# Layer 0's adaLN modulation: shift and scale by fp32 products at the start, the other 32 column tiles inside the attention

## The reference, cut to what matters

```python
def adaln(cond, w, b):
    m = (jax.nn.silu(cond) @ w + b)[..., None, :]
    return jnp.split(m, 6, axis=-1)          # w: 1024 x 6144, fp32, 25 MB
...
        mp = adaln(c_ctx, ada_w[layer], ada_b[layer])    # 128 context tokens
        ms = adaln(c, ada_w[layer], ada_b[layer])        # 512 latent tokens
        hp = modulate(yp, mp[0], mp[1])                  # x * (1 + scale) + shift
        hs = modulate(ys, ms[0], ms[1])
        if kind == 0:                                    # layers 0 and 3: latent attention
            op, ckv, kpe = mla_context(hp, *wts)
            os_ = mla_latent(hs, cache_ckv[:, j], cache_kpe[:, j], cos, sin, *wts)
        ...
        yp = layer_norm(ALPHA * yp + mp[2] * op, ln_g[layer, 0], ln_b[layer, 0])
        fp = swiglu(modulate(yp, mp[3], mp[4]), ffn_wg[layer], ffn_wu[layer], ffn_wd[layer])
        yp = layer_norm(ALPHA * yp + mp[5] * fp, ln_g[layer, 1], ln_b[layer, 1])
```

## Time and profile before

| | us |
|---|---|
| median of 3 runs | 3951.5 |
| the three runs | 3951.24, 3951.50, 3957.62 |
| span of the profiled execution | 3955.7 |

### The profile page before, as it was taken

The page is one execution under the profiler, slowest core; times in us unless marked ns, Lnnn a source line. Parts: engine busy times, 40 slices in busy tenths (PEclk is TensorE's granted clock), DMA queues, the critical chain, the costliest instruction groups (busy, mean ns, idle before and its releaser), DMA issues.

```text
span 3955.7 us, 74569 instructions
## 1 busy us (share of the span) xinstructions
PE 3625.6 (92%) x31532; PEld 3412.5 (86%) x31532; DVE 2466.1 (62%) x3517; ACT 938.1 (24%) x1804; POOL 1840.3 (47%) x875
## 2 busy tenths in 40 slices
PE   8999999999889778888999994899999989999998
PEld 3877799999788678888999994799998777899997
DVE  5366678758785466655885768886676566632125
ACT  5322231001244255532310012310013222220011
POOL 1311156665455646535566552466554101356663
PEclk9999999999999888889999997899999999999999
DMA  8200024333235543322343331243332000122221
GB/s 318 62 12 17 17 81 147 136 112 123 70 127 182 149 87 94 84 55 102 114 142 119 124 101 36 90 145 128 123 102 73 27 12 17 43 70 75 76 76 53
DMA packets 226844, 367.60 MB, mean 93 GB/s; under 512 B 104752, under 2 KB 111088, under 8 KB 226416
## 3 DMA queue, kind: packets, MB, share of 16 engines
q1 hardware_dynamic: 171408, 255.08, 20.9%
q10 hardware_dynamic: 55136, 107.98, 7.9%
HBM read 326.47 MB, written 36.54 MB: 92 GB/s over the span
## 4 chain that ended last, share of the span: by engine, by line
PE 71%; DVE 16%; issue 3%; ACT 3%; DMA 1%; SPq 1%; POOL 1%; ACTq 1%; DVEq 0%; POOLq 0%
PE ps L819 52%; PE ps L1091 3%; PE ps L1067 3%; DVE f_acc L2159 2%; PE ps L862 2%; PE ps L1077 2%; DVE m_mx L2390 1%; PE ps L1046 1%; DVE r_t L2456 1%; DVE x L2257 1%; DVE r_hlo L2440 1%; DVE ps L2605 1%; PE ps L1027 1%; DVE x L2266 1%; PE ps L879 1%
## 5 line engine op out<-in xcount | busy, mean ns | idle before, releaser
L674 POOL TENSOR_TENSOR w_hi<-w_raw,zrow 128x1024 fp32r<-128x1024 f32 x354 | 693.7, 1959 | 1783.6 <-PE ps L819 979.9
L676 POOL TENSOR_TENSOR w_lo<-w_raw,w_hi 128x1024 fp32r<-128x1024 f32 x354 | 900.2, 2543 | 27.8
L2159 DVE SCALAR_TENSOR_TENSOR f_acc<-f_unit,silu_c,f_acc 128x512 f32<-128x512 f32 x504 | 631.3, 1293 | 7.6
L819 PE MATMUL ps<-f_hhi,w_hi 128*128 128x320 f32 x2688 | 634.1, 317 | 0.0
L819 PE MATMUL ps<-f_hhi,w_lo 128*128 128x320 f32 x2688 | 613.0, 309 | 0.0
L819 PE MATMUL ps<-f_hlo,w_hi 128*128 128x320 f32 x2688 | 610.8, 308 | 0.0
L819 PEld LDWEIGHTS ps<-f_hlo,w_hi 128*128 128x128 f32 x2688 | 449.6, 188 | 0.0
L819 PEld LDWEIGHTS ps<-f_hhi,w_lo 128*128 128x128 f32 x2688 | 448.9, 188 | 0.0
L819 PEld LDWEIGHTS ps<-f_hhi,w_hi 128*128 128x128 f32 x2688 | 441.2, 188 | 0.0
L819 PE MATMUL ps<-f_ahi,w_hi 128*128 128x320 f32 x1408 | 322.2, 310 | 0.2 <-DVE f_alo L2304 0.2
L819 PE MATMUL ps<-f_alo,w_hi 128*128 128x320 f32 x1408 | 320.9, 309 | 0.0
(11 more groups left out here) (401 smaller groups left out, 6710.4 us busy)
## 6 DMA issues: line engine op xcount, KB each, us to landing
w_raw<-in_w SPq DMA_DIRECT2D x340, 512.0 KB, 3.5
f_unit<-in_ada_w ACTq DMA_DIRECT2D x72, 1024.0 KB, 5.8
ada_ring<-in_ada_w SPq DMA_DIRECT2D x24, 1024.0 KB, 6.6
up_scratch<-r_o ACTq DMA_DIRECT2D x40, 320.0 KB, 3.3
s_LW<-up_scratch SPq DMA_DIRECT2D x16, 320.0 KB, 5.1
s_LA<-up_scratch SPq DMA_DIRECT2D x8, 640.0 KB, 6.6
x<-in_x SPq DMA_DIRECT2D x1, 2560.0 KB, 9.4
x_scratch<-r_o ACTq DMA_DIRECT2D x8, 320.0 KB, 2.2
```

What stands on the lines that cost most here:

```text
L674: nc.gpsimd.tensor_tensor(whi[:, slot, :], raw[:, raw_slot, :], zrow[:, 0:1].to_broadcast([P, CH * P]), ALU.add).then_inc(w_hi_done, 1)
L676: nc.gpsimd.tensor_tensor(wlo[:, slot, :], raw[:, raw_slot, :], whi[:, slot, :].bitcast(F32), ALU.subtract).then_inc(w_split, 1)
L819: last = mm(ps[:, 2 * b + h, 0:HT], w, r[:, h * HT:(h + 1) * HT], start=kt == 0 and n < 2, stop=kt == KT - 1 and n >= 4)
L2159: last = stt(acc[:, cd, :], unit[:, k, :], by, acc[:, cd, :], ALU.mult, ALU.add)
```

## The change

The opening loads only the first 2048 of the matrix's 6144 columns (shift and scale): 8 units, each with its own buffer. They are not split: PE uses them as the stationary operand in plain fp32, 128 x 128 each, with silu(c), 2 columns wide, moving; that gives the result as columns and needs no turning. DVE adds the bias (and 1 to the scale), and ACT waits for that (`ada_mod`) and for x (`s_x`); the three barriers at the start are gone. x is loaded behind the 8 units and the first weight chunk.

The other 4096 columns are 32 tiles of 128 columns, four for each pair of the attention, each with 8 fp32 products (`late`). ACT issues their loads of 512 KB: three at the pair's beginning, the fourth after the first tile's products. PE multiplies tile 0 of a pair before `turn(0)`, tile 1 before `turn(5)`, tile 2 before `turn(9)` and tile 3 before `av(9)`. DVE copies the pair's 8 result columns behind its last copy of a transpose. `modulation(0)` runs on DVE after the loop.

```diff
-ADA_SLOTS, ADA_SPLITS = 4, 3
+EARLY = 2 * KD // 4
+LATE_AT = 2 * KD
+LATE_GROUPS = 4
+LATE_BUFFER = (0, 0, 1, 2)
+LATE_TURN, LATE_AV = (0, 5, 9), (10,)
...
             sp.dma_start(cst[:, :], a["cst"]).then_inc(s_const, 16)
-            sp.dma_start(x[:, :, :], a["x"].rearrange("k p t -> p k t")).then_inc(s_const, 16)
...
-            for u in range(ADA_UNITS):
-                slot = u % ADA_SLOTS
-                if u >= ADA_SLOTS:
-                    sp.wait_ge(ada_lo, u - ADA_SLOTS + 1)
-                sp.dma_start(m_ada.ring[slot][:, :, :],
+            for u in range(2 * EARLY):
+                sp.dma_start(m_ada.unit[u][:, :, :],
                              src[:, 4 * (u % 2):4 * (u % 2) + 4, (u // 2) * 512:(u // 2 + 1) * 512]
-                             ).then_inc(ada_land[slot], 16)
+                             ).then_inc(ada_land[u // 2], 16)
...
+                    pieces(LAYER_BASE[L], order, 0, 1)
+                    if L == 0:
+                        sp.dma_start(x[:, :, :], a["x"].rearrange("k p t -> p k t")).then_inc(s_x, 16)
+                    pieces(LAYER_BASE[L], order, 1)
...
-                for n in range(48):
-                    mm(ps[:, 6, 2 * n:2 * n + 2], m.rows[0:2, n * P:(n + 1) * P], ident[0:2, 0:2], start=True, stop=True)
-                end()
-                end()
+                pe.wait_ge(s_cond, 1)
+                for cb in range(EARLY):
+                    units = m_ada.unit[2 * cb:2 * cb + 2]
+                    pe.wait_ge(ada_land[cb], 32)
+                    for n in range(4):
+                        for k in range(KD):
+                            last = mm(ps[:, 6, 8 * cb + 2 * n:8 * cb + 2 * n + 2], units[k // 4][:, k % 4, n * P:(n + 1) * P],
+                                      sc_c[:, k, :], start=k == 0, stop=k == KD - 1)
+                last.then_inc(ada_mm, 1)
+
+            def late(j, p):
+
+                b = LATE_BUFFER[p]
+                pe.wait_ge(ada_land[b], j * 32 + 16 * (p + 3) if b == 0 else j * 16 + 48)
+                for k in range(KD):
+                    last = mm(ps[:, 7, 2 * p:2 * p + 2], m_mla[0].late[b][:, k, :], sc_c[:, k, :], start=k == 0, stop=k == KD - 1)
+                last.then_inc(late_mm, 1)
...
+                        if L == 0 and u in LATE_TURN:
+                            late(j, LATE_TURN.index(u))
                         if u < 10:
                             turn(u)
+                        if L == 0 and u in LATE_AV:
+                            late(j, len(LATE_TURN) + LATE_AV.index(u))
                         if u:
                             av(u - 1)
...
+                    act.wait_ge(s_x, 16)
+                    act.wait_ge(ada_mod, 1)
...
+                    act.dma_start(m.late[LATE_BUFFER[p]], late_src[:, :, bass.ds(j * (LATE_GROUPS * P) + (LATE_AT + p) * P, P)]
+                                  ).then_inc(ada_land[LATE_BUFFER[p]], 16)
...
+                    if L == 0:
+                        for p in (0, 2, 3):
+                            load_late(j, p)
                     for u in range(10):
                         qt = u % 5
+                        if L == 0 and u == LATE_TURN[0] + 2:
+                            act.wait_ge(late_mm, j * LATE_GROUPS + 1)
+                            load_late(j, 1)
...
+                ch(tt(mod[:, 0:LATE_AT, :], ps[:, 6, 0:2 * LATE_AT].rearrange("p (n c) -> p n c", c=2),
+                      adab[:, 0, 0:LATE_AT].unsqueeze(2).to_broadcast([P, LATE_AT, 2]), ALU.add))
+                s = mod[:, KD:2 * KD, :]
+                ts(s, s, 1.0, None, ALU.add).then_inc(ada_mod, 1)
...
+                    if L == 0:
+                        dve.wait_ge(late_mm, j * LATE_GROUPS + LATE_GROUPS)
+                        cp(mods[0][:, bass.ds(j * LATE_GROUPS + LATE_AT, LATE_GROUPS), :],
+                           ps[:, 7, 0:2 * LATE_GROUPS].rearrange("p (n c) -> p n c", c=2))
```

More of the change, by code:

```diff
@@ L241, in build @@
         sc_c = sb("silu_c", [P, KD, 2])
-        sc_hi, sc_lo = sb("silu_hi", [P, KD, 2], F32R), sb("silu_lo", [P, KD, 2], F32R)
         hmod, hmix = sb("hmod", [P, 2, KD, 2]), sb("hmix", [P, 2, KD, 2])
@@ L270, in build @@
         stage_end = sem("stage_end")
-        stage_free = sem("stage_free")
-        s_init, s_const = sem("s_init"), sem("s_const")
-        ada_land = [sem(f"ada_land{i}") for i in range(ADA_SLOTS)]
+        s_init, s_const, s_x, s_cond, s_eps = sem("s_init"), sem("s_const"), sem("s_x"), sem("s_cond"), sem("s_eps")
+        ada_land = [sem(f"ada_land{i}") for i in range(EARLY)]
         unit_land = [sem(f"unit_land{i}") for i in range(2)]
         unit_used, unit_sum, unit_col = sem("unit_used"), sem("unit_sum"), sem("unit_col")
-        ada_mm, ada_row, ada_hi, ada_lo = sem("ada_mm"), sem("ada_row"), sem("ada_hi"), sem("ada_lo")
+        ada_mm, ada_mod, late_mm = sem("ada_mm"), sem("ada_mod"), sem("late_mm")
         outs_done = sem("outs_done")
@@ L289, in f_ada @@
         def f_ada(m, g):
-            m.rows = g("ada_rows", [2, 6 * D])
-            m.hi, m.lo = ([g(f"ada_{n}{i}", [P, 4, 512], F32R) for i in range(ADA_SPLITS)] for n in ("hi", "lo"))
-            m.ring = [g(f"ada_ring{i}", [P, 4, 512]) for i in range(ADA_SLOTS)]
+            m.unit = [g(f"ada_unit{i}", [P, 4, 512]) for i in range(2 * EARLY)]
         def f_ffn(L):
@@ L334, in f @@
                 m.mx = g(f"m_mx{L}", [P, 2])
+                if L == 0:
+                    spare = m.t32.rearrange("p a t -> p (a t)")[:, 0:KD * P].rearrange("p (k n) -> p k n", k=KD)
+                    m.late = [g(f"m_late{b}", [P, KD, P])[:, :, :] for b in range(2)] + [spare]
             return f
@@ L657, in _ @@
                 elif MIXER[L] == 0:
-                    pieces(LAYER_BASE[L], [[(c, 0, CH)] for c in MLA_IN])
+                    order = [[(c, 0, CH)] for c in MLA_IN]
+                    pieces(LAYER_BASE[L], order, 0, 1)
+                    if L == 0:
+                        sp.dma_start(x[:, :, :], a["x"].rearrange("k p t -> p k t")).then_inc(s_x, 16)
+                    pieces(LAYER_BASE[L], order, 1)
                     stream(LAYER_BASE[L] + C_MLA_IN, LAYER_BASE[L + 1])
@@ L1506, in pooling @@
                 spread(2 * L)
-            pe.wait_ge(s_const, 32)
-            end()
             for L in range(DEPTH):
@@ L1521, in _ @@
             af = nc.scalar.activation
[L1523 to L1536, removed]
             def load_unit(L, h):
@@ L2087, in pooling @@
                        scale=lna[:, 1, 0, kt:kt + 1]).then_inc(q.xs, 1)
[L2090 to L2094, removed]
+            act.wait_ge(s_const, 16)
+            act.wait_ge(s_eps, 1)
+            af(sc_c[:, :, :], cond, ACT.Silu).then_inc(s_cond, 1)
             for L in range(DEPTH):
-                if L == 0:
-                    ada()
                 (mla, rwkv, pooling)[MIXER[L]](L)
@@ L2112, in ada @@
             def ada():
[L2113 to L2121, removed]
+                dve.wait_ge(ada_mm, 1)
+                mod = mods[0]
+                ch(tt(mod[:, 0:LATE_AT, :], ps[:, 6, 0:2 * LATE_AT].rearrange("p (n c) -> p n c", c=2),
+                      adab[:, 0, 0:LATE_AT].unsqueeze(2).to_broadcast([P, LATE_AT, 2]), ALU.add))
+                s = mod[:, KD:2 * KD, :]
+                ts(s, s, 1.0, None, ALU.add).then_inc(ada_mod, 1)
             def modulation(L):
                 mod = mods[L % 2]
-                ch(tt(mod[:, :, :], mod[:, :, :], adab[:, L, :].unsqueeze(2).to_broadcast([P, 48, 2]), ALU.add))
-                for part in (1, 4):
+                n0 = 0 if L else LATE_AT
+                ch(tt(mod[:, n0:48, :], mod[:, n0:48, :], adab[:, L, n0:48].unsqueeze(2).to_broadcast([P, 48 - n0, 2]), ALU.add))
+                for part in (1, 4) if L else (4,):
                     s = mod[:, part * KD:(part + 1) * KD, :]
@@ L2406, in mla @@
                 end()
+                if L == 0:
+                    modulation(0)
                 out_proj(L, mods[L % 2][:, 2 * KD:3 * KD, :])
@@ L2779, in _ @@
             nc.vector.memset(eps[:, 2:3], GN_EPS)
[L2780 to L2784, removed]
+            nc.vector.memset(eps[:, 3:5], 0.0).then_inc(s_eps, 1)
             for L in range(DEPTH):
```

3 lines of the change are left out of this document (2 added, 1 removed).

## The result

The changed kernel takes 3970.45 us (median of 4 executions, 3963.43 to 3975.03), the kernel before 3951.37 (4 executions, 3947.86 to 3957.62): a ratio of 1.0044, 95% interval 1.003 to 1.0058. It is 0.4% slower. The forecast was 3968.

The account below looks back on a forecast made before the run. TensorE was taken to bound the kernel, leading the chain with 71% of the span. Opening -43.2, late tiles +34, copy +0.7 and clock +25 give +16.5 us: 3968 us, range 3946 to 3982.

Parts of the forecast that it names:

- The opening: Start of layer 0: 256 records at half clock take 54.6 us; first panel at 68.0 instead of 111.22, gain 43.2 us.
- Rival (b): Opening runs at full clock: products take 28.5 us instead of 54.6, first panel at 42, time 3942; chance 0.05.
- The late tiles at full clock: Attention: 32 tiles of 1.78 us make 57.0 us, of which 23 us fall into TensorE's waits; +34 us.
- the copy: Behind each pair DVE copies 8 result columns ahead of the scaling, at most 0.1 us late; +0.7 us.
- The clock at the pair ends: Half-clock falls at all eight pair ends, reaching into the fourth tile, 4.2 us each, less 8.4 now: +25 us.
- rival (a): Pair ends: clock behaves as before, no more or earlier falls; time 3943, deciding at 8.5 us extra loss; chance 0.09.
- (c): Falls at every pair end but late, 2.4 to 3.3 us each: +11 to +18, time near 3957; chance 0.18.
- Rival (d): Tile before turn(5) brings mid-pair falls too: 8 more of 1.7 us, +14, time 3982; chance 0.10.
- The loads: Late tiles' 512 KB loads take 3.5 us, turn(0) is 9.5 us on; even doubled they stay hidden.
- rival (e): Late loads land late because of small pieces, TensorE waits at turn(0): 2 us x 8, time 3984; chance 0.03.
- The sum: Whole program: -43.2 + 34 + 0.7 + 25 = +16.5 us; 3968 us against the median of 3951.5, 0.4% slower.

Follow-up runs that it names:

- e6: Changed kernel with the opening's products moving 64 columns instead of 2, no wide matmuls ahead; 3960.7 us (one execution).
- e5: Changed kernel with eight 320-column fp32 matmuls of constants ahead of the opening's products, which stay 2 columns wide; 3963.0 us (one execution).
- e9: Changed kernel with only late tiles 2 and 3 of each pair moving 64 columns instead of 2; 3936.9 us (one execution).
- e1: Changed kernel with all late tiles' products moving 64 columns instead of 2; 3931.8 us, ratio 0.9956 to the kernel before.
- e10: Changed kernel with only late tiles 0 and 1 of each pair moving 64 columns instead of 2; 3965.5 us (one execution).
- e7: Changed kernel with the late tiles placed before turn(0), turn(3), turn(5) and turn(7), none at a pair's end; 3959.3 us, ratio 1.0036 to the kernel before.
- e3: Changed kernel with late and opening products moving 64 columns, and eight wide matmuls ahead of the opening's products; 3910.73 us, ratio 0.9899 to the kernel before.
- e2: Changed kernel with eight wide matmuls ahead of the opening's products, and those products moving 64 columns; 3944.0 us, ratio 0.9985 to the kernel before.

## Why the prediction was right, point by point

**The opening: right, term by term.** Predicted: 256 records at 0.213 us, 54.6 us, TensorE done at 64.3, ACT at 64.9, the first panel at 68.0. Measured 54.74 busy, last start 64.0, ACT at 64.91, panel at 67.77; −43.4 for −43.2. The carrying step was to take the price from the turning's rows at half clock and to hold that thin products do not raise the clock. e6 shows that thinness was not the whole reason: products of 64 columns did not raise it either. Rival (b) is out. One detail was wrong: the granted clock was to show 0.50. The window of the opening shows it as 1.00 over 9.6 to 64.4, since no level is recorded in this trace before 73.0 us; 0.50 stands only behind a recorded fall, as in e5, with the same 353 ns records. At a program's start the spacing of records tells the clock, not the printed value.

**The late tiles at full clock: right, 2 us too high.** The loop without its clock losses is 298.4 − 8.4 = 290.0 before, and by e9 (half of 3.24 us lost) 324.1 − 1.6 = 322.5; e1 gives 325.3 − 2.8 = 322.5 (half of the 5.68 us that PE worked at half clock). So products and copy cost about 32.4 for 34.7. From start to start a tile takes 1.70 to 1.79 us in these two kernels, not 1.78 throughout; that makes about 1 us of the difference. The cover was there: TensorE's waits in the loop are now

```profile
PE ps L1110 <- DVE m_O L2380: 3.6, 8, 0.5
PE ps L1047 <- issue: 2.6, 1, 2.6
PE ps L821 <- DVEq L476: 2.0, 1, 2.0
PE ps L1047 <- ACTq L476: 1.0, 1, 1.0
```

and the 16 waits for the exponent and those for `m_PT` are gone. The waits for the turned output are the eight of 3.6 us together that stood there before, 0.45 in the earlier trace rows, so the copy, for which 0.7 was put in, costs nothing.

**The clock at the pair ends: right in place and kind, 2 us too high.** Falls at all eight ends, each over the fourth tile, none in mid pair, as forecast. Extra cost 55.1 − 32.4 = 22.7 for 25. Half the time that TensorE worked in the eight stretches, less 8.4, makes 26: the counting by which I worked comes out 3 us too high, probably by the part that falls into waits, which no run shows by itself. The steady end costs 4.3 (43.9 against 39.6 in e1), for the 4.2 taken. e1 shows that it is the clock and nothing else, e9 and e10 that it is the tiles at the end; both were only argued in the prediction. With that rival (a) is out, whose point of decision was 8.5 us of extra loss, and so is (c), with 11 to 18. Rival (d) did not happen here; e7 shows falls in mid pair, though behind another tile.

**The loads: right.** The earlier trace rows had 3.5 us for 512 KB. DMA issues of after (KB each, median us from issue to landing):

```profile
m_late<-in_ada_w ACTq DMA_DIRECT2D x24, 512.0 KB, 4.3
...
m_t<-in_ada_w ACTq DMA_DIRECT2D x8, 512.0 KB, 6.7
```

No wait of TensorE ends with a load; rival (e) is out. `modulation(0)` behind the loop costs nothing: output projection to FFN takes 72.1 us after and 72.0 before.

**The sum.** By its terms: −43.2 + 34 + 0.7 + 25 = +16.5 was forecast; −43.4 + 32.4 + 22.7 = +11.7 came, and the profiles show 11.9. Between the medians lie 19.1 (11.9 to 22.9 by the interval). The difference between 19.1 and 11.9 need not be layer 0's: the unchanged rest of the program varies by 12.5 us between the traces, and the profiled execution of before (3957.62) lay 6 us above its median, that of after on it. Which part it comes from is not shown for executions without a trace. The prediction had that 6 as 4, because it held the span of 3955.7 against the median of times. The forecast of 3968 for 3970.45 is thus nearer than its terms were, and in part luck: they were 5 us too high together, and the executions lay 7 us higher. Why the rest varies was not settled; its half-clock stretches add up to 296 to 330 us and do not follow its length.

## What to carry to other kernels

Products with a few moving columns cost more than their own time when they stand among other narrow work: here 32 tiles of 1.75 us, 56 us of which 23 fell into old waits, cost 32 us themselves and 23 us more in what runs at half clock. Where the load of the stationary operand sets the pace, as it did here, widening the moving operand by a broadcast cost next to nothing (1.78 against 1.75 us per tile of 8) and the clock held: +0.4% became −0.4% (e1), and −1.0% with the opening widened too and eight wide matmuls ahead of it (e3). Moving the thin tiles elsewhere was no substitute here, since new falls came with them (e7).

## What was not expected of the hardware

- Over products of 64 moving columns a clock that was up held (e2, 28 us at 0.112 us per record), and one that was down did not rise (e6, 54.5 us at 0.213).
- Once down, the clock stayed down for 17.1 us of gapless narrow work and scores in mid pair (e7), while ten of the loop's thirteen stretches were 3.4 us.
- DVE's `m_hlo` takes 2.2 us instead of 0.83 while POOL splits weights (e3), and POOL's splits grow by up to 0.6 us.
